# Join and projection after a mixture of experts: the first tile's two gathers issued one phase earlier, and VectorE's first steps in another order

## What is computed

```python
# end of the first block
x = x + gate_f * hierarchical_moe(h, ...)          # per token: the rows of its two experts, weighted
x = rms_norm(x, final_g)
# start of the second block
h = rms_norm_2(x, norm_mix) * (1 + sc_m) + sh_m
proj = h @ w_in                                    # q, k, v of 16 heads and the forget logits
```

## Time and profile before

| | |
|---|---|
| median of 3 runs | 2510.35 us (2507.32 to 2511.96) |
| the profiled execution | 2508.33 us, its span 2506.7 us |
| granted TensorE clock, mean | 0.99 |
| busy | PE 96%, DVE 76%, ACT 54%, POOL 24% of the span |
| experts' phase ends, attention starts | about 1181 and 1182 us of the span |
| join of the eight tiles | about 1182 to 1262 us |
| rest of the attention phase | to about 1742 us |

### The profile page before, as it was taken

How to read it: one execution, slowest core, us unless ns; L and a number is a source line. 1 busy time by engine, 2 the same in 40 slices (tenths; PEclk the granted TensorE clock), 3 DMA queues, 4 the chain that set the end, 5 groups by cost and what they waited for, 6 DMA issues and landing times. The chain is left out here.

```text
span 2506.7 us, 33887 instructions
## 1 busy us (share of the span) xinstructions
PE 2411.3 (96%) x11957; PEld 1983.4 (79%) x11957; DVE 1916.6 (76%) x2471; ACT 1354.0 (54%) x1914; POOL 590.1 (24%) x495
## 2 busy tenths in 40 slices
PE   7999999899999999999799999998999999999999
PEld 4766678678888888787589999997788888788887
DVE  4876678678989888997788888887767666657786
ACT  3242323357777777775576766776434444444332
POOL 2000354143333233332621111110042333300000
PEclk8999999999999999999999999999999999999999
DMA  7778356589878899997721111112332443587874
GB/s 260 220 246 285 110 204 216 227 311 397 337 271 308 306 397 400 387 406 296 241 61 51 51 52 52 51 39 113 132 110 86 158 161 139 187 308 265 299 255 151
DMA packets 181316, 535.36 MB, mean 214 GB/s; under 512 B 17711, under 2 KB 77715, under 8 KB 167881
## 3 DMA queue, kind: packets, MB, share of 16 engines
q1 hardware_dynamic: 163900, 470.20, 51.6%
q0 software_dynamic: 12592, 45.63, 4.8%
q10 hardware_dynamic: 4700, 17.92, 1.8%
HBM read 443.38 MB, written 90.33 MB: 213 GB/s over the span
## 5 line engine op out<-in xcount | busy, mean ns | idle before, releaser
L1754 PE MATMUL psum<-w_high,block_hT_high 128*128 128x512 f32 x576 | 232.4, 404 | 7.1 <-DVE w_low L1368 5.4
L1368 DVE TENSOR_TENSOR w_low<-first_w_up,w_high 128x2048 fp32r<-128x2048 f32 x72 | 186.0, 2621 | 53.4 <-ACT w_high L1362 53.4
L1756 PE MATMUL psum<-w_high,block_hT_low 128*128 128x512 f32 x576 | 225.2, 391 | 0.0
L1755 PE MATMUL psum<-w_low,block_hT_high 128*128 128x512 f32 x576 | 224.8, 390 | 0.0
L1754 PE MATMUL psum<-w_qkv_high,fox_hT_high 128*128 128x384 f32 (+1 forms) x512 | 182.1, 356 | 12.7 <-DVE v_high_low L2647 5.2
L1368 DVE TENSOR_TENSOR w_low<-first_w_gate,w_high 128x2048 fp32r<-128x2048 f32 x74 | 169.3, 2291 | 17.7 <-ACT w_high L1362 17.5
L1754 PE MATMUL psum<-w_mlp_out_high,hidden_part_high 128*128 128x512 f32 x448 | 175.6, 392 | 3.7 <-DVE hidden L3979 3.2
L1468 POOL TENSOR_TENSOR block_out<-block_out,late_rows 128x1024 f32<-128x1024 f32 x35 | 92.4, 2640 | 357.7 <-ACT block_out L1633 357.7
L1362 ACT ACTIVATE w_high<-first_w_gate 128x2048 fp32r<-128x2048 f32 x74 | 141.2, 1912 | 64.2 <-DMA first_w_gate<-in_w_expert_gate 55.1
L1755 PE MATMUL psum<-w_mlp_out_low,hidden_part_high 128*128 128x512 f32 x448 | 175.2, 391 | 0.0
L1756 PE MATMUL psum<-w_mlp_out_high,hidden_part_low 128*128 128x512 f32 x448 | 175.1, 391 | 0.0
(11 more groups left out here) (514 smaller groups left out, 6745.2 us busy)
## 6 DMA issues: line engine op xcount, KB each, us to landing
first_w_gate<-in_w_expert_gate SPq DMA_DIRECT2D x32, 2048.0 KB, 10.0
first_w_up<-in_w_expert_up SPq DMA_DIRECT2D x32, 2048.0 KB, 10.3
first_w_down<-in_w_expert_down SPq DMA_DIRECT2D x31, 2048.0 KB, 16.4
w_mlp_out_quarters<-in_w_mlp_out SPq DMA_DIRECT2D x78, 512.0 KB, 7.0
hidden_part<-hidden_parts SPq DMA_DIRECT2D x54, 512.0 KB, 4.4
v_aug<-in_w_ada SPq DMA_DIRECT2D x48, 512.0 KB, 5.5
expert_rows<-block_out POOLq DMA_DIRECT2D x34, 512.0 KB, 8.7
v_aug<-in_ada_w SPq DMA_DIRECT2D x32, 512.0 KB, 4.6
```

Source lines behind the costliest of these rows:

```text
L1368: dve.tensor_tensor(wl[:, par, half], raw[kind][:, half], wh[:, par, half].bitcast(F32), ALU.subtract).then_inc(s_wl, 1)
L1754: pe.matmul(out, sh, mh, start=start, stop=False)
L1755: pe.matmul(out, sh, ml, start=False, stop=False)
L1756: return pe.matmul(out, sl, mh, start=False, stop=stop)
```

## The change

1. The two buffers of gathered rows get a fixed place and exist in both phases, and so do their four semaphores.
2. At the end of its program in the experts' phase GpSimd waits for the last two stores (`s_last` at 32) and issues tile 0's two gathers there. `gather(0)` is gone from its program in the attention phase.
3. In VectorE's program `first_result(0)`, `second_result(0)` and `final_scaled(0)` stand ahead of the low shift part and of `low_weights(0)`, and `scaled_rows(0)` and `low_weights(0)` stand ahead of `final_scaled(1)`.

```diff
+RESULTS = 196096
...
+            results = [nc.alloc_sbuf_tensor_at(f"result{i}", [P, 2, D], F32, offset=RESULTS + 8 * D * i) for i in range(2)]
+            gathered = [[nc.alloc_semaphore(f"result{i}{u}_gathered") for u in range(2)] for i in range(2)]
...
                     pool.wait_ge(s_x[0], n_pairs * 16 + 16)
                     pool.sem_inc(s_own, 1)
+                    pool.wait_ge(s_last, 32)
+                    for k in range(2):
+                        pool.indirect_dma_start(results[k][:, 0, :], None, moe_dram,
+                                                bass.IndirectOffsetOnAxis(ap=rows_i[:, k, 0:1], axis=0)).then_inc(gathered[k][0], 16)
...
-                r0 = sbuf(early, "result0", [P, 2, D])
-                r1 = sbuf(early, "result1", [P, 2, D])
+                sbuf(early, "result_space", [P, 4, D])
+                r0, r1 = results
...
-            s_g = [[sem(f"j_gather{k}{u}") for u in range(2)] for k in range(2)]
...
-                    gather(0)
                     gather(1)
                     gather(2)
                     rstd(0)
...
-                    dve.wait_ge(s_ch, 1)
-                    dve.tensor_tensor(shift_parts[32:32 + KT, :], bank[6][32:32 + KT, 0:P], shift_parts[32:32 + KT, :].bitcast(F32), ALU.subtract).then_inc(s_cl, 1)
-                    low_weights(0)
                     first_result(0)
                     second_result(0)
                     final_scaled(0)
+                    dve.wait_ge(s_ch, 1)
+                    dve.tensor_tensor(shift_parts[32:32 + KT, :], bank[6][32:32 + KT, 0:P], shift_parts[32:32 + KT, :].bitcast(F32), ALU.subtract).then_inc(s_cl, 1)
                     first_result(1)
                     second_result(1)
+                    scaled_rows(0)
+                    low_weights(0)
                     final_scaled(1)
-                    scaled_rows(0)
                     first_result(2)
```

More of the change, by code:

```diff
@@ L122, in build @@
             cm = sbuf(xs, "causal_bf16", [P, P], BF16)
-            phase(moe, x1_dram, normed_dram, moe_dram, late, rows_i, gate2, w_qkv, idb, cm, picks, chosen, first_raw, first_in)
-            phase(attention, x1_dram, moe_dram, x2_dram, f_dram, heads_dram, late, rows_i, gate2, w_qkv, idb, cm, stored, gated, grow, o_ahead, w_ahead, picks, shift_parts, free=False)
+            results = [nc.alloc_sbuf_tensor_at(f"result{i}", [P, 2, D], F32, offset=RESULTS + 8 * D * i) for i in range(2)]
+            gathered = [[nc.alloc_semaphore(f"result{i}{u}_gathered") for u in range(2)] for i in range(2)]
+            phase(moe, x1_dram, normed_dram, moe_dram, late, results, gathered, rows_i, gate2, w_qkv, idb, cm, picks, chosen, first_raw, first_in)
+            phase(attention, x1_dram, moe_dram, x2_dram, f_dram, heads_dram, late, results, gathered, rows_i, gate2, w_qkv, idb, cm, stored, gated, grow, o_ahead, w_ahead, picks, shift_parts, free=False)
         phase(fox_out_mlp, place, x2_dram, heads_dram, x3_dram, parts, stored, gated, grow, o_ahead, w_ahead, out)
@@ L1247, in _, with moe @@
                         ins.then_inc(c_h, 1)
-def moe(nc, a, sbuf, sem, psum, bank, ident, ones, mhalf, mods, x1_dram, normed_dram, moe_dram, late, rows_i, gate2, w_qkv, idb, cm, picks, chosen, first_raw, first_in):
+def moe(nc, a, sbuf, sem, psum, bank, ident, ones, mhalf, mods, x1_dram, normed_dram, moe_dram, late, results, gathered, rows_i, gate2, w_qkv, idb, cm, picks, chosen, first_raw, first_in):
     gl8, gm8, em8, oh, mem, io = chosen
@@ L1756, in split_mm, with attention @@
     return pe.matmul(out, sl, mh, start=False, stop=stop)
-def attention(nc, a, sbuf, sem, psum, bank, ident, ones, mhalf, mods, x1_dram, moe_dram, x2_dram, f_dram, o_dram, late, rows_i, gate2, w, idb, cm, s_st, s_wg, grow, o_ahead, w_ahead, picks, shift_parts):
+def attention(nc, a, sbuf, sem, psum, bank, ident, ones, mhalf, mods, x1_dram, moe_dram, x2_dram, f_dram, o_dram, late, results, s_g, rows_i, gate2, w, idb, cm, s_st, s_wg, grow, o_ahead, w_ahead, picks, shift_parts):
     w_pk = a["fox_w_in_2"][0].rearrange("(p k) n -> p k n", k=KT)
```

## The result

| | before | after |
|---|---|---|
| median of 14 runs each, in turn | 2511.76 us (2502.69 to 2522.49) | 2519.2 us (2512.95 to 2529.43) |
| ratio | 1 | 1.0035, 95% interval 1.0022 to 1.0048 |
| the profiled execution | 2508.33 us, span 2506.7 | 2516.76 us, span 2515.1 |
| granted TensorE clock, mean | 0.990 | 0.987 |

A forecast was written before the change was run, and what follows sets the result against it. TensorE, busy 96% of the span, bounds the kernel, and the join is a chain through all engines. First product 3.5 us late plus clock 1.5 gives 5.0: profiled 2508.3 becomes 2513.3, median 2515.4 us, range 2509.5 to 2520.5.

The forecast's parts named there:

- The barrier between the phases: End of the experts' phase: GpSimd issues two gathers before arriving, so every engine enters the attention phase 2.5 us later.
- Rival 2: End of the experts' phase opens only once GpSimd's gathers have landed, attention phase 4 us later still: 2519.4 us; chance 0.11.
- The gathers: Tile 0's gathers, issued at 1181.3 instead of 1182.9, land 5.1 us later; first_result(0) gains 1.6 us.
- Tile 0 on VectorE, and what was moved behind it: VectorE's list in the join: scaled_rows(0) 1.7 us earlier, final_scaled(1) 3.6 later, scaled_rows(1) 1.6 later.
- weights(1) and the forget bias: SyncE's queue: weights(1) issued 8.6 us later; with the forget bias, first product 1.6 to 5.4 us late, 3.5 taken.
- rival 1: Join: late transfers hidden by less crowding, only VectorE's 1.6 us stays, clock kept up: 0 to +2 us, 2511.4; chance 0.2.
- TensorE's clock: First product: after some 8 us idle, one stretch at half clock costs 1.5 us.
- The sum: End of the join, and so of the kernel: 3.5 + 1.5 = 5.0 us later, median 2515.4 us.
- The first paragraph: Behind the join TensorE works 463 of 480 us, so the kernel's end moves by what the join's end moves.

## Why the prediction was wrong, point by point

- **The barrier between the phases: the step that failed.** "Every engine enters the attention phase 2.5 us later" was 9.8. The 2.5 itself was right, 2.6 from the store's landing to the last descriptor. What was missing, a cost put at nothing, is the drain behind it, 7.4 us from the last descriptor to its end. The prediction counted GpSimd as arrived once its second gather was written, and took its 10.5 idle us for free time; the line that ends the phase has a drain of 8363 ns in the trace of before. I read busy rows and waits, and a drain is neither.
- **Rival 2, the barrier that waits for the gathers' data**, came near in its time (2519.4 us, measured 2519.2) with a chance of 0.11, and that was luck for the larger part. Its phase starts 6.7 us late (1189), the measured one 9.8. A wait alone, without any gather, already costs 6.0 of the 9.8, and the drain ended 3.1 us behind the landing, not with it. Whether the drain waits for data at all is open. The rule that I let speak against this rival, of the Trainium skill, page "Perfetto Trace Analysis", section "DMA Instruction — SWDGE (GPSIMD)", is about the gather's own instruction, and holds for it (1.03 and 0.95 us here); it says nothing of a drain behind it, and I used it as if it did.
- **The gathers.** Landing 5.2 us after the issue of the second (forecast 5.1). first_result(0) did not gain 1.6 us but lost 4.0, by the barrier alone: without the drain it gains 2.1.
- **Tile 0 on VectorE, and what was moved behind it.** Without the drain scaled_rows(0) is 1.65 us early (forecast 1.7), final_scaled(1) 3.6 late (3.6), scaled_rows(1) 1.5 late (1.6). rstd(1) took 1.5 us. These terms were right; in the change they lie under the barrier.
- **weights(1) and the forget bias.** The forecast let them hold the first product to +3.5, between bounds of 1.6 and 5.4. They held nothing: `low_weights(1)` and `low_forget` waited for neither, since issues and landings fell from 8.9 and 7.1 us to 4.1 and 3.4. That half of rival 1 was right: without the drain the first product is 1.5 us late, VectorE's own list. (With `low_weights(0)` alone behind, they do cost, 0.84 us.) What was late instead is `store(0)`, behind them in the queue, and final_scaled(2) with it, 1.7 us. The prediction had store(0) in the list of what moves and gave it no price.
- **TensorE's clock.** One stretch at 0.50 on the first product was right in place and wrong in number: two more follow, where the kernel before has one behind its first product. Yet from the first product to the end of the join the change takes only 1.1 us longer (54.7 against 53.6), the wait for `store(0)` included, where the forecast had 1.5 for one stretch. Near in size, then, but not for its reason; no run of the change with the clock kept up was made.
- **The sum.** Order, weights and clock were put at 5.0 us; the order alone moved the end of the join by 4.2 and the time by 0.18%, 4.5 us (0.5 to 8.5 by the interval). The size held, 2.8 at the first product (3.5 forecast) and 1.4 behind it (1.5), but the 2.8 were VectorE's own list and not the weights. The barrier's 9.8 us, of which tile 0's landed rows give back 2.1 by the first product, lift it to 8.8.
- **The first paragraph**, that the end moves by what the end of the join moves, held: 8.8 us there, 8.4 in the span, 8.8 in the ratio; that the last is the same to the tenth is chance, its interval being 5.5 to 12.

## What to carry to other kernels

Before you give an engine work at the end of a phase, look at what it does there that is not busy time: a drain that ended 2.6 us ahead of the barrier cost nothing until two short instructions and a wait were put in front of it, and then it cost all of its length. Price such a move by the engine that becomes the last to arrive, its drain included (here about 0.08 us for each transfer GpSimd has issued in the phase), and if the work must be there, let the engine drain first, while it is idle: that took the phase's start from 15.1 to 11.8 us after the anchor, though not back to 5.3. And where filling matmuls keep the clock up, fit them again when the waits around them move: otherwise the half-clock stretch, harmless on a filling before, falls on the products.

## What the runs showed of the hardware that I had not expected

- GpSimd's drain at the end of this phase takes 6.0 to 6.3 us even when its last work is a wait (6.04), a copy of one column (6.27) or a transfer whose data has landed (6.20). Its length goes with the number of transfers that GpSimd issued since the last drain, about 0.08 us each: 6.04 us for 73, 6.20 for 75, and at the end of the attention phase 1.4 for 16 and about 1.2 for 14.
- Of GpSimd's drains behind gathers in flight, those at the end of the phase ended 3.1 us behind the landing (two kernels) or 0.13 us behind it (with a drain ahead), while the one ahead of the semaphore clearing ended 0.13 us behind the last descriptor and some 4 us ahead of the landing. A drain in a listing is not by itself a sign that data has landed.
- The drains of the other engines in the barrier that follows take 7 ns (SyncE), 8 (ScalarE), 13 (TensorE) and 19 (VectorE), and GpSimd's there 40. The Trainium skill, page "VectorE: DVE Perf Modes", section "The DRAIN you can't avoid", gives about 12 ns on all five engines for drains ahead of and behind a kernel. Those here stand inside it and are no case of that rule: the barrier's are of that size or up to three times it (GpSimd's), GpSimd's at the end of the phase is 6 us and more.
- The same three transfers of `weights(1)` take 8.9 us to land beside the gathers of the first tiles and 4.1 us behind them, and the issue of the forget bias 2.95 us or 0.68. In the change, to issue them later was no delay, up to the point at which a store stood behind them. What they stand beside is the only difference that the traces show, and no run varied it alone.
